# Routed experts two at a time: plain fp32 weights on the two column halves of TensorE, and nineteen landing places

## The reference, cut to what matters

```python
g_gate, g_idx = lax.top_k(softmax(t @ w_rg + b_rg), 1)          # one of 4 groups
e_w, e_idx = lax.top_k(softmax(e_logits of that group), 2)      # two of its 8 experts
hid = silu(t @ w1[e]) * (t @ w3[e])                             # 1024 -> 256
y += weight[e] * (hid @ w2[e])                                  # 256 -> 1024
x = x + y
```

## Time and profile before

| | |
|---|---|
| Time, median of 3 runs | 1543.88 us (1542.98 to 1547.75) |
| Span of the profiled execution | 1548.3 us |
| PE busy | 1435.4 us (93%) |
| DVE busy | 904.7 us (58%) |
| ACT busy | 745.6 us (48%) |
| POOL busy | 134.4 us (9%) |
| Moved by DMA | 205.99 MB, 133 GB/s on average |

### The profile page before, as it was taken

How to read it: one execution, slowest core, us unless ns; L and a number is a source line. 1 busy time by engine, 2 the same in 40 slices (tenths; PEclk the granted TensorE clock), 3 DMA queues, 4 the chain that set the end, 5 groups by cost and what they waited for, 6 DMA issues and landing times.

```text
span 1548.3 us, 18556 instructions
## 1 busy us (share of the span) xinstructions
PE 1435.4 (93%) x7643; PEld 1165.3 (75%) x7643; DVE 904.7 (58%) x1272; ACT 745.6 (48%) x1088; POOL 134.4 (9%) x87
## 2 busy tenths in 40 slices
PE   6999999999999976999999949999979879999998
PEld 5888886678667866888888738778869666678887
DVE  3445237854785567989998748567475353312253
ACT  4334244455444254989988745344221256622231
POOL 0000000000000002444344310000000000000000
PEclk9999999999999986999999979999999989999999
DMA  6222321113224347999999732101010030003231
GB/s 222 92 83 80 101 92 55 55 55 109 82 72 150 148 167 290 370 358 381 380 384 378 250 117 82 55 28 55 1 55 1 28 109 27 1 28 105 86 136 55
DMA packets 67792, 205.99 MB, mean 133 GB/s; under 512 B 9604, under 2 KB 10742, under 8 KB 55415
## 3 DMA queue, kind: packets, MB, share of 16 engines
q1 hardware_dynamic: 61810, 194.21, 34.6%
q0 software_dynamic: 5760, 10.50, 2.7%
q10 hardware_dynamic: 132, 0.03, 0.0%
HBM read 196.33 MB, written 16.78 MB: 138 GB/s over the span
## 4 chain that ended last, share of the span: by engine, by line
PE 71%; DVE 12%; DMA 9%; ACT 6%; issue 1%; POOL 0%; SPq 0%; DVEq 0%; POOLq 0%; ACTq 0%
PE PS L506 16%; PE PS L508 15%; PE PS L507 15%; PE PS L969 4%; PE PS L503 4%; DMA x_scratch<-work,slot_tokens 3%; DVE wlo L1212 3%; PE PS L1137 2%; PE PS L820 2%; PE PS L821 2%; DMA raw<-in_w 2%; ACT whi L2057 2%; PE PS L1128 2%; ACT work L2057 2%; DVE smalls L1204 1%; PE PS L1153 1%
## 5 line engine op out<-in xcount | busy, mean ns | idle before, releaser
L1212 DVE TENSOR_TENSOR wlo<-raw,whi 128x2048 fp32r<-128x2048 f32 x90 | 206.0, 2288 | 300.8 <-ACT whi L2057 300.7
L2057 ACT ACTIVATE whi<-raw 128x2048 fp32r<-128x2048 f32 x90 | 171.9, 1910 | 252.2 <-PE PS L508 227.0
L506 PE MATMUL PS<-whi,hthi 128*128 128x512 f32 x480 | 195.5, 407 | 7.1 <-DVE wlo L1212 5.3
L506 PE MATMUL PS<-hthi,whi 128*128 128x512 f32 x480 | 198.0, 412 | 0.8 <-DVE htlo L1245 0.8
L508 PE MATMUL PS<-hthi,wlo 128*128 128x512 f32 x480 | 188.7, 393 | 0.0
L507 PE MATMUL PS<-htlo,whi 128*128 128x512 f32 x480 | 188.3, 392 | 0.0
L508 PE MATMUL PS<-whi,htlo 128*128 128x512 f32 x480 | 188.0, 392 | 0.0
L507 PE MATMUL PS<-wlo,hthi 128*128 128x512 f32 x480 | 188.0, 392 | 0.0
L2057 ACT ACTIVATE work<-PS 128x512 f32<-128x512 f32 (+4 forms) x176 | 79.6, 462 | 98.7 <-PE PS L508 34.5
L2057 ACT ACTIVATE scratch<-PS 128x512 f32<-128x512 f32 (+4 forms) x116 | 58.0, 507 | 134.8 <-PE PS L503 57.0
L506 PEld LDWEIGHTS PS<-hthi,whi 128*128 128x128 f32 x480 | 91.1, 190 | 32.5 <-issue 14.1
(11 more groups left out here) (367 smaller groups left out, 2721.8 us busy)
## 6 DMA issues: line engine op xcount, KB each, us to landing
raw<-in_w_in SPq DMA_DIRECT2D x44, 1024.0 KB, 5.1
raw<-in_w SPq DMA_DIRECT2D x44, 1024.0 KB, 12.2
scratch<-in_w SPq DMA_DIRECT2D x26, 1024.0 KB, 9.7
merged<-in_w SPq DMA_DIRECT2D x26, 1024.0 KB, 10.9
raw<-in_w_gate SPq DMA_DIRECT2D x8, 1024.0 KB, 5.0
raw<-in_w_out SPq DMA_DIRECT2D x8, 1024.0 KB, 5.2
raw<-in_w_up_a SPq DMA_DIRECT2D x6, 1024.0 KB, 4.9
raw<-in_w_up_b SPq DMA_DIRECT2D x6, 1024.0 KB, 5.0
```

What stands on the lines that cost most here:

```text
L506: e.matmul(o, lh, rh, start=start, stop=False)
L1212: tt(lo, raw_place(j), as_f32(hi), SUB).then_inc(*ve.mark("lo", j))
L2057: return e.activation(o, i, f, bias=bias, scale=scale)
```

## The change

Expert m and expert m + 16 are worked on together, 16 pairs. Their 64 tokens each stand side by side: 128 gathered rows, turned into 128 columns; the first expert's tokens load columns 0 to 63 of the array and write partitions 0 to 63 of the result, the second's columns 64 to 127 and partitions 64 to 127. The weights stay fp32 and are read where they landed; nothing of the experts is split, and hi and lo tokens are gone. The sum is scaled by the token's weight before `down`, by DVE. ACT and DVE each copy one half of tokens and results.

Since whi, wlo, hthi, htlo, yhi and ylo hold no expert parts, they are landing places now: nineteen in all. A place of the experts is free when PE has read the unit (`pe["unit", j]`). The stores of x1 move from SP's queue to POOL's, those of xn to ACT's, so that SP's queue holds only loads there. POOL gathers two pairs ahead.

```diff
+    def pair_up(m):
+        unit["up", m] = len(units), 4
         for w in (w1, w3):
...
+            for n in pair_of(m):
+                units.append([(lambda a: a.rearrange("p (k f) -> p k f", k=KD),
+                               w[0, n].rearrange("(p k) f -> p k f", k=KD))])
+
+    def pair_down(m):
+        unit["down", m] = len(units), 2
+        for n in pair_of(m):
+            units.append([(lambda a: a.rearrange("p (k n) -> p k n", k=2),
+                           w2[0, n].rearrange("(p k) n -> p k n", k=2))])
...
+    y_slots = [y_plain[:, n // 2, HB * (n % 2):HB * (n % 2) + HB, :].rearrange("p k n -> p (k n)") for n in range(4)]
+    slots = [raw[:, n, :] for n in range(NR)]
+    slots += [w_plain[:, n, :] for n in range(2 * NS)] + [h_plain[:, n, :] for n in range(4)] + y_slots
+    slots += [m_all[:, n * UNIT:(n + 1) * UNIT] for n in range(2)]
+    slots += [T[:, BANK + n * UNIT:BANK + (n + 1) * UNIT] for n in range(2)]
+    W_SLOT, H_SLOT = NR, NR + 2 * NS
+    Y_SLOT = H_SLOT + 4
+    M_SLOT, T_SLOT = Y_SLOT + 4, Y_SLOT + 6
+    landing_order = [Y_SLOT, Y_SLOT + 1, Y_SLOT + 2] + [(MOE + n) % NR for n in range(NR)]
+    landing_order += [*range(W_SLOT, Y_SLOT), Y_SLOT + 3, *range(M_SLOT, len(slots))]
+
...
-        raw_slot[j] = j % NR if j < MOE + 2 else (j - MOE - 2) % (NR + LENT_RAW) if j < TWO else \
+        raw_slot[j] = j % NR if j < MOE else landing_order[(j - MOE) % len(slots)] if j < TWO else \
...
+        def up(m, a):
+
+            u, j = m % 2, unit["up", m][0] + 2 * a
+            ps = fresh("up", m, a)
+            w = [raw_place(j + x).rearrange("p (k f) -> p k f", k=KD) for x in range(2)]
+            on.wait_ge(*ac["out", "bring", m, 0])
+            on.wait_ge(*ve["out", "bring", m, 1])
+            for x in range(2):
+                on.wait_ge(*raw_got[raw_slot[j + x]][j + x])
...
-            for k in range(KD):
-                e.matmul(ps, TOK[u][:, k, :], wh[:, k, :], start=k == 0, stop=False)
-                m = e.matmul(ps, TOK[u][:, k, :], wl[:, k, :], start=False, stop=k == KD - 1)
...
+                for x in range(2):
+                    rows_ = slice(x * CAP, x * CAP + CAP)
+                    t = e.matmul(ps[rows_, 0:DE], TOK[:, u, k, rows_], w[x][:, k, :], start=k == 0, stop=k == KD - 1)
+            t.then_inc(*pe.mark("up", m, a))
+            for x in range(2):
+                pe.also("unit", j + x)
+            bank.filled(("up", m, a))
+
...
+        def down(m):
+
+            u, j = m % 2, unit["down", m][0]
...
                 for k in range(2):
-                    m = e.matmul(pv[:, a, k, :], UP[:, n % 2, a, k::2], pairs, start=True, stop=True)
...
+                    for x in range(2):
+                        rows_ = slice(x * CAP, x * CAP + CAP)
+                        t = e.matmul(ps[rows_, :], HT[:, u, k, rows_], w[x][:, k, cols], start=k == 0, stop=k == 1)
+                t.then_inc(*pe.mark("down", m, half))
+                bank.filled(("down", m, half))
+            for x in range(2):
+                pe.also("unit", j + x)
...
+            for x in range(2):
+                pe.also("unit", j + x)
 
         bring(0)
-        for n in range(NE + 1):
-            if 0 < n < NE - 1:
-                bring(n + 1)
-            if n < NE:
-                up(n, 0)
-                if n == 0:
-                    bring(1)
-                up(n, 1)
-            if n:
-                down(n - 1)
-            if n < NE:
-                hand_over(n)
+        for m in range(PAIRS):
+            up(m, 0)
+            if m:
+                hand_over(m - 1)
+            else:
+                bring(1)
+            up(m, 1)
+            if m:
+                down(m - 1)
+                if m + 1 < PAIRS:
+                    bring(m + 1)
+        hand_over(PAIRS - 1)
+        down(PAIRS - 1)
...
         split()
-        split()
+        assert next_unit[0] == MOE
+        next_unit[0] = TWO
...
+        def gated(m):
+            u = m % 2
+            on.wait_ge(*ac["sigmoid", m])
+            tt(SG[:, u, :], SG[:, u, :], inside("up", m, 0)[:, 0:DE], MUL).then_inc(*ve.mark("out", "up", m, 0))
+            on.wait_ge(*pe["up", m, 1])
+            if m > 1:
+                on.wait_ge(*pe["hidden", m - 2])
+            settle()
+            stt(HID[:, u, :], SG[:, u, :], info[:, m:m + 1], inside("up", m, 1)[:, 0:DE], MUL, MUL).then_inc(
+                *ve.mark("out", "up", m, 1))
+            ve.also("hid", m)
...
+        for i in range(NT):
+            on.wait_ge(*ac["n2", "xs", i])
+            e.dma_start(xn_dram[i * P:i * P + P, :], xs[:, i, :]).then_inc(*xn_put.mark())
+        xn_put.also("all")
         on.wait_ge(*ve["ex"])
         act(ex, ex, ACT.Exp).then_inc(*ac.mark("ex"))
-        split()
...
-        for _ in range(LENT_SPLIT):
-            split()
...
+        def half_tokens(m):
+            on.wait_ge(*pe["bring", m, 0])
+            if m > 1:
+                on.wait_ge(*pe["up", m - 2, 1])
+            act(TOK[:, m % 2, 0:HB, :], inside("bring", m, 0).rearrange("p (k n) -> p k n", k=HB), ACT.Copy).then_inc(
+                *ac.mark("out", "bring", m, 0))
+
+        def gate_half(m):
+            on.wait_ge(*pe["up", m, 0])
+            if m > 1:
+                on.wait_ge(*ve["hid", m - 2])
+            act(SG[:, m % 2, :], inside("up", m, 0)[:, 0:DE], ACT.Sigmoid).then_inc(*ac.mark("sigmoid", m))
+
+        def hidden(m):
+            on.wait_ge(*pe["hidden", m])
+            if m > 1:
+                on.wait_ge(*pe["down", m - 2, 1])
+            act(HT[:, m % 2], inside("hidden", m)[:, 0:2 * P].rearrange("p (k n) -> p k n", k=2), ACT.Copy).then_inc(
+                *ac.mark("out", "hidden", m))
+
+        def half_rows(m):
+            if m > 1:
+                on.wait_ge(*yo_put[m - 2])
+            on.wait_ge(*pe["down", m, 0])
+            act(YO[:, m % 2, 0:BANK], inside("down", m, 0), ACT.Copy).then_inc(*ac.mark("out", "down", m, 0))
+
+        half_tokens(0)
+        for m in range(PAIRS):
+            gate_half(m)
+            if m:
+                hidden(m - 1)
+            else:
+                half_tokens(1)
+            if m:
+                half_rows(m - 1)
+                if m + 1 < PAIRS:
+                    half_tokens(m + 1)
+        hidden(PAIRS - 1)
+        half_rows(PAIRS - 1)
...
+        for c in range(HB):
+            on.wait_ge(*ve["out", "wo", 1, c])
+            e.dma_start(x2_dram[c * P:c * P + P, :], x1[:, c, :]).then_inc(*x1_put.mark())
+        x1_put.also("all")
...
+            if m > 1:
+                on.wait_ge(*pe["bring", m - 2, 1])
...
+            if m:
+                on.wait_ge(*yo_put[m - 1])
...
+        for m in range(2):
+            gather(m)
+        for m in range(PAIRS):
+            if m + 2 < PAIRS:
+                gather(m + 2)
+            add_rows(m)
...
-            if raw_prior[j] is not None and raw_prior[j] < LATE <= j and raw_slot[j]:
-                on.wait_ge(*pe["turned", "kb" if raw_slot[j] == 2 else "qb", 0, HB - 1])
-            elif raw_prior[j] is not None:
...
+            s, prior = raw_slot[j], raw_prior[j]
+            if prior is None:
+                if Y_SLOT <= s < M_SLOT:
+                    on.wait_ge(*pe["ub", 1, HB - 1])
+                    if s == Y_SLOT + 3:
+                        on.wait_ge(*ve["gain", NT - 1])
+                elif W_SLOT <= s < Y_SLOT:
+                    on.wait_ge(*pe["wo", 1, HB - 1])
+                elif M_SLOT <= s < T_SLOT:
+                    on.wait_ge(*x1_put["all"])
+                    on.wait_ge(*ve["gain", NT - 1])
+                elif s >= T_SLOT:
+                    on.wait_ge(*ve["overflow"])
+                    on.wait_ge(*pe["info weights"])
+            elif MOE <= prior < TWO:
+                on.wait_ge(*pe["unit", prior])
+            elif prior < LATE <= j and s:
+                on.wait_ge(*pe["turned", "kb" if s == 2 else "qb", 0, HB - 1])
+            else:
+                on.wait_ge(*ve["lo", prior])
             for place, src in units[j]:
                 e.dma_start(place(raw_place(j)), src).then_inc(*raw_got[raw_slot[j]].mark(j))
...
-        for j in range(first_out + NR, MOE + NR):
-            load(j)
-
-
-        for c in range(HB):
-            on.wait_ge(*ve["out", "wo", 1, c])
-            e.dma_start(x2_dram[c * P:c * P + P, :], x1[:, c, :]).then_inc(*x1_put.mark())
-        x1_put.also("all")
-        for i in range(NT):
-            on.wait_ge(*ac["n2", "xs", i])
-            e.dma_start(xn_dram[i * P:i * P + P, :], xs[:, i, :]).then_inc(*xn_put.mark())
-        xn_put.also("all")
-        for j in range(MOE + NR, TWO + NR):
+        for j in range(first_out + NR, TWO + NR):
             load(j)
```

More of the change, by code:

```diff
@@ L320, in build @@
     MOE = len(units)
[L321 to L325 removed]
+    for m in range(PAIRS + 1):
+        if m < PAIRS:
+            pair_up(m)
+        if m:
+            pair_down(m - 1)
     TWO = len(units)
@@ L826, in hand_over @@
-        def hand_over(n):
```

(45 more changed lines are left out.)

349 lines of the change are left out of this document (121 added, 228 removed).

## The result

The changed kernel takes 1504.24 us (median of 4 runs, 1502.79 to 1505.38), beside it the kernel before 1543.44 us: ratio 0.9746, 95% interval 0.9734 to 0.9759. The forecast was 1498 us. By the medians 39.2 us are gone, where 46 were forecast. From profile to profile the span went from 1548.3 to 1501.0 us, 47.3 less; each profile is one execution, before's well above the median of its kernel, after's the shortest of four. What follows goes by the profiles.

What follows compares the result with a forecast made beforehand. Weight loads were taken to bound the expert stage, PE close behind. Release 607, stream 232 and tail 17 put the reload at 856 us, 46 less: 1502 us profiled, 1498 timed; own range 1483 to 1515, wide range 1455 to 1540.

Steps and rivals of the forecast that it cites:

- The bound: Expert stage: weight loads are the bound, PE is close behind, and a queue of adds is left at the end.
- first release: Twentieth expert load, waiting until the first up product has read unit 0: about 607 us, bounds 601.5 and 615.
- The sum: Start of the x2 reload after the experts: 607 + 232 + 17 = 856 us against 902.3, 46 us less.
- the stream: The 77 remaining expert weight units at 3.01 us each, 232 us; last landing near 839 us.
- the end: From the last unit's landing through the last product and adds to the x2 reload: 17 us, bounds 11 and 25.
- The landing of nineteen units: Before the expert products: 32 us of loads and 6 us for stores from 561 us, all in at about 601 us.
- PE: Expert products: two column halves run at once, 12.6 us a pair, hidden under 18.1 us of loads.
- The sign that PE would wait for DMA in a third of the plateau: Expert stage after the change: PE busy 12.6 of 18.1 us a pair, otherwise waiting on DMA.
- The other end, 22.6: Expert products if column halves run one after the other: 22.6 us a pair, PE the bound, 1616 us; chance 0.16.
- The stores: xn and x2 leave on ACT's and POOL's queues: xn lands near 584 us and delays nothing, or near 594 in one line.
- The traffic of q0 is kept: Expert gathers and adds: the same 1024 rows are moved, in 32 transfers instead of 64.
- Early loads: Before the expert products: 19 landing places instead of 7, so 19 units in at about 601 us against about 7.

Runs made afterwards that it cites:

- in turn: The changed kernel with all records of the first expert's column half before all of the second's, instead of alternating: 1551.99 us, ratio 1.0043 to the kernel before.
- the two runs with 2 rows: The changed kernel with 2 rows instead of 128 per gather from the third pair on (1493.42 us), or per add (1473.46 us).

## Why the prediction was right, point by point

- *The bound.* Right: but for a dip about the first release the engines are full from 561 us, and with half the bytes the time falls.
- *The sum.* It was right to 0.5 us partly by luck: the first release came 2.7 us late, the stream took 4.1 us less than forecast, the end 0.9 more. Its range is narrower than its terms: their bounds, added up, give 1477 to 1520 us, not 1483 to 1515.
- *The landing of nineteen units.* 606.65 us, predicted 601 (its terms, 561 + 32 + 6, make 599). Of the thirteen from 561 us on, five landed 3.7 to 3.8 us apart beside the stores; over 2.48 each that is some 6 us, the lump that was counted for them. Not counted: the first took 5.2 us from its issue to its landing, and four later ones landed 3.2 to 3.9 us apart, three of them beside the first gathers.
- *First release.* 609.68, predicted 607. The gather landed at 600.5 as predicted, but by two misses that cancel: the token indices were ready at 592.1 us and not at 589.5, and the gather landed 7.5 us after its start, for which, with its work on POOL, I had 9.9. Most of the indices' delay is a term that I had put at nothing: the router's 16 records for them take 3.6 us where before's, with half the columns (64 of 128), take 1.9. The stores on ACT account for some 0.5 us; by so much the indices are earlier, from the first load on, with the stores on SP. The first product took 6.32 us at the lower clock, for which I had some 5.
- *The stream.* 77 units from 609.68 to 837.59 are 2.96 us each, predicted 3.01. The row of the same mixture was the right one to take: a unit alone lands in 2.48, which leaves some 37 us for the 77, and 8.4 and 20.9 of these are the gathers and adds of q0, by the two runs with 2 rows. What the other 8 are was not taken apart.
- *PE.* Halves together, as taken from the row halves; 13.1 us a pair at full clock, predicted 12.6. The sign that PE would wait for DMA in a third of the plateau did not come: it is busy 188 of 220 us. With nineteen units ahead it does sixteen pairs while 77 units land, 14.6 us a pair, and only from 796 us on does it wait for weights for long (3.6, 1.4 and 2.8 us). The other end, 22.6, would have been too dear even in turn: 18.3.
- *End.* 17.9 us from the last unit to the reload, predicted 17, by the path that was predicted: the add of the pair before and the last add behind it (8.0 and 5.4 us, predicted 8.1 and 6.2). What the prediction had not seen is that the first of them hangs on `down` of pair 14, and so on a unit that landed at 832.58, not on the last. In before it had the last unit at 868 and an end of 34 us, from the fall of the share; the unit landed at 875.33, the end was 26.9. Neither enters the sum, but the gain is 38 and 9 us and not 29 and 17.
- *What was costed at nothing.* The stores: right in the end. The last piece of xn landed at 587.9 us, between the 584 and the 594 of the prediction and ahead of the indices. "The traffic of q0 is kept", in 32 transfers instead of 64: right for the stream, wrong as a price of nothing. With 32 adds again, and the gathers behind them, the whole gain is lost. I had read the earlier trace rows as adds that fall behind after the last load; but they wait for each other well before it, from 801.81 us on. Before's longest wait from 760 to 902 us (us in total, times, longest) is one add for the landing of the one before:

```profile
POOL x_scratch L2688 <- DMA x_scratch<-work,slot_tokens: 40.0, 8, 6.4
```

  With gathers two ahead, half as many adds is a condition of the gain, not a detail. The kernel before with its adds halved and nothing else was not tried.
- *Early loads.* The prediction counted about a dozen more units landed by 601 us; they are worth 24 to 27 us at the last unit and not 38, since they also hold up the first gather. How the rest of the gain, some 40%, divides between the faster unit and the shorter end was not measured apart.
- *Profile and median.* 1502 was forecast for the profile, 1501.0 came. The 1498 was wrong by 6 us because I carried the 4.4 us between before's profile and its median over to after; after's profile lies 3.2 us below its own median. So the forecast of the profile was nearer than that of the median, and how before's stage looks in an execution nearer to its median is not shown.

## What to carry to other kernels

When a resource is full, count everything that runs through it: here the adds of about 4 MB held back the weights by 20.9 us, in which nearly 9 MB of weights land at 2.48 us a unit. A transfer that must wait for the one before it is a chain with a time per transfer, so fewer and taller ones are worth more than their bytes say. And where two halves of the array are to run together, write their products alternately.

## What the runs showed of the hardware that was not expected

Two column halves of the array ran fp32 products at twice the rate of one: two records in 0.215 us where one half alone took 0.215 a record; out of order in the program they met only over about three records at each change of half. An add of up to 64 rows landed in a median of 7.4 us, one of up to 128 in 9.8, one of two rows in 5.8: more than half of its time does not hang on its rows. (Beside the adds of 64 rows the queue of loads was shorter, 10.7 to 13.1 us from issue to landing against 27 to 31 in after, so that row is not like for like.) Loads that landed 2.48 us apart alone landed 3.7 apart beside stores from two other queues.
